# State-space stage: conditioning weights spread by 1 MB units over the rounds, x for the norms in 4 KB packets, a tile's outputs ahead of the next tile's lags

## Chip, cores and metric

One NeuronCore of a Trainium2 chip runs the kernel. The metric is device time in microseconds (us) of one execution, median of several runs. Engines: TensorE (PE), VectorE (DVE), ScalarE (ACT), GpSimd (POOL), and SyncE (SP), which only issues DMAs here.

## What is computed

Two transformer-like blocks over 256 tokens of width 2048, in f32. The change touches only the first mixer of the first block, a state-space layer, and the conditioning ahead of it:

```python
def adaln(cond, w, b):
    return jnp.split(jax.nn.silu(cond) @ w + b, 6, axis=-1)      # w_mod: 2048 x 12288
...
sh1, sc1, gt1, sh2, sc2, gt2 = adaln(c, w_mod[layer], b_mod[layer])
csh1, csc1, cgt1, csh2, csc2, cgt2 = adaln(c_ctx, w_mod[layer], b_mod[layer])
h_lat = modulate(rmsnorm(x_lat, norm_mix_pre[layer]), sh1[:, None], sc1[:, None])
h_ctx = modulate(rmsnorm(x_ctx, norm_mix_pre[layer]), csh1, csc1)
...
lam_bar, b_bar = s5_discretise(...)
st_ctx = s5_scan(uc_ctx, lam_bar, b_bar, s0, reverse)
st_lat = s5_scan(uc_lat, lam_bar, b_bar, s_ctx_final, reverse)
y_lat = y_lat + jnp.einsum('btgp,ghp->btgh', st_lat, c_mat).real   # both directions
```

`x_lat` (x) and `x_ctx` (ctx) have 256 rows each. The gelu of y_lat goes into the GLU matmul, and from there on the kernel is a sequence of large matmuls that the change leaves alone.

## The kernel before

**Tiles and rounds.** The 2048 channels are 16 tiles (KT) of 128. For each tile the recurrence is cut into chunks of L = 8 tokens: inside a chunk a Toeplitz matrix of lags (`tw`), between chunks a scan over states. Software pipeline, one tile per round: `for k in range(-1, KT)` on TensorE and ACT, `for k in range(KT)` on VectorE, `for n` on GpSimd and SP. Every engine's order is written out by hand, and semaphores tie them.

**One round on TensorE** (L1310 to L1340): `lag_blocks(k+1)` (L1247, needs GpSimd's `cpow` of tile k+1), `states(k+1)` (L1263), `outputs(k)` (L1277 with `tw`, L1280 with the states), two units of conditioning weights in `ada_rows` (L1188), `spread_modulation`, `select_c` (L1179), `transpose_x` (L1221), `output_transposes(k)` (L1290), two `transpose_e` (L1234) with two more units between them, and in rounds 0 to 3 four units more (`mod_rows`). `mod_columns` (L1199) turns a finished row of conditioning into columns.

**The others.** GpSimd: `powers_of_c(n)` (into `cpow`, two buffers; waits for `outputs(n-2)` through y_done) and `phases(n)` (into `pt`), all through the helper at L1841; before tile 2 it scales the remaining powers of lambda. VectorE: `rotate(k)` (phase rotation and scan, gives s_done), `copy_lags(k+1)` (L1717 to L1719, into `rw`), `finish`, in three rounds `modulation` (L1731 and neighbours), `powers_of_b(k+2)`; most through the helper at L1539. ACT: the gelu (L1454), PSUM copies, `modulate_u` (L1442), `normalise_x` (L1432), and it issues the weights of the rounds (L1078). SP: `toeplitz(n)` stores `rw` to DRAM (L1108), waits, and loads it back as `tw` by eight DMAs (L1113; `tw` has one buffer, so it also waits for `outputs(n-1)`), then loads C (L1099) and x (L1103) for tile n+3.

**Conditioning weights.** w_mod (2048 x 12288) comes as 24 blocks of 512 columns, each in 4 units of 1 MB ([128, 4, 512]), through the 4 slots of `raw`. Block 0 to 3 (16 units) are worked off ahead of the rounds, round -1 takes 4 units, rounds 0 to 3 take 8 each, rounds 4 to 14 take 4 each. A unit's load waits until the unit four earlier is used (ada_unit).

**Prologue.** `load_xs` brings x and ctx rows for the norms in two halves of four tokens, onto 64 partitions (32 for each of ctx and x, 8 KB runs); ACT squares them with accumulation (`square_x`, L1392, 8 instructions), VectorE and ACT make rstd_x from them. VectorE builds the lambda powers (lp_ready), `powers_of_b(0)`, the phase table ab[2,3], `modulation(0)`, a complex product (`cmul`), the table ab[0,1], and gives tables_ready (L1761), which GpSimd's `phases(0)` needs.

## Time and profile before

| | |
|---|---|
| median of 3 runs | 3557.34 us (3548.33 to 3568.26) |
| profiled execution: time, span | 3554.54 us, 3552.7 us |
| mean granted TensorE clock | 0.955 of 2.4 GHz |
| busy over the span | PE 3286.0 us (92%), DVE 2145.0 (60%), ACT 1380.7 (39%), POOL 480.5 (14%) |
| DMA | 643.22 MB, mean 181 GB/s |
| state-space stage | 0 to about 465 us |

The profile is one execution. The page gives totals over the whole span; the stage is some 13% of it, so its rows come from the trace, cut to stretches. L numbers are lines of the kernel before. In a row, "[3.73 <-PE acc L1247]" says that the engine sat idle for 3.73 us before it, and what ended that. A DMA's time to landing runs from its issue.

### The profile page before, as it was taken

To read this page: it belongs to the slowest core of one execution; us is meant where nothing else is said; L and a number is where in the kernel's file an instruction comes from. 1 tells how busy PE (TensorE), PEld (TensorE's weight loads), DVE (VectorE), ACT (ScalarE), POOL (GpSimd) and SP (SyncE) were. 2 spreads that over 40 slices of the span, in tenths; PEclk is the share of its full clock that TensorE was granted. 3 is DMA by queue.
4 is the path that set the end of the run, shared out by engine and by line. 5 is a ranking of instruction groups with operands and counts; after the bars stand their busy time and mean duration, and the time that the engine had idled before them with its cause. 6 is when DMAs were issued, how large, how long until landed. Compare 5 with 4: busy or idle time off the path is not lost.

```text
span 3552.7 us, 51801 instructions
## 1 busy us (share of the span) xinstructions
PE 3286.0 (92%) x21097; PEld 2763.3 (78%) x21097; DVE 2145.0 (60%) x1850; ACT 1380.7 (39%) x1385; POOL 480.5 (14%) x352
## 2 busy tenths in 40 slices
PE   5788899799999999886789999999999899999998
PEld 3445578688888888675678888888868788888887
DVE  7668755565555555699565555555644555555555
ACT  4446543433333333322234434433323344344332
POOL 2869900000000000096000000000000000000000
PEclk7888899899999999998799999999999999999999
DMA  9988875255555555344145555555524455555552
GB/s 299 305 282 257 260 243 175 91 184 189 185 189 182 190 186 189 107 142 148 36 154 178 186 190 182 186 189 189 177 92 142 142 186 184 187 187 189 189 183 89
DMA packets 351014, 643.22 MB, mean 181 GB/s; under 512 B 21599, under 2 KB 50359, under 8 KB 350519
## 3 DMA queue, kind: packets, MB, share of 16 engines
q1 hardware_dynamic: 309952, 561.68, 48.9%
q10 hardware_dynamic: 40951, 79.98, 6.6%
q8 instruction: 80, 1.31, 0.2%
q14 instruction: 31, 0.25, 0.0%
HBM read 637.54 MB, written 4.06 MB: 181 GB/s over the span
## 4 chain that ended last, share of the span: by engine, by line
PE 83%; DVE 6%; POOL 5%; issue 2%; DMA 2%; ACT 1%; SPq 1%; DVEq 1%; ACTq 0%; POOLq 0%
PE acc L439 49%; PE acc L440 25%; POOL cpow L1841 3%; DMA raw<-in_w_mod_dram 2%; POOL ptmp L1841 1%; PE acc L1263 1%; DVE z L943 1%; DVE w_lo L793 1%; PE acc L1280 1%; PE acc L521 1%; PE acc L533 1%; PE acc L464 1%; PE acc L1188 1%; PE acc L1247 1%; DVE hf L832 0%
## 5 line engine op out<-in xcount | busy, mean ns | idle before, releaser
L439 PE MATMUL acc<-xin,w_hi 128*128 128x512 f32 x5376 | 1915.2, 399 | 58.9 <-DVE xin L807 33.7
L793 DVE TENSOR_TENSOR w_lo<-raw,w_hi 128x2048 fp32r<-128x2048 f32 x484 | 1111.2, 2301 | 1079.0 <-ACT w_hi L640 1078.8
L440 PE MATMUL acc<-xin,w_lo 128*128 128x256 f32 x5376 | 1519.4, 283 | 0.0
L640 ACT ACTIVATE w_hi<-raw 128x2048 fp32r<-128x2048 f32 x484 | 926.8, 1917 | 1365.1 <-PE acc L440 1365.0
L439 PEld LDWEIGHTS acc<-xin,w_hi 128*128 128x128 f32 x5376 | 1017.2, 189 | 312.5 <-issue 35.6
L440 PEld LDWEIGHTS acc<-xin,w_lo 128*128 128x128 f32 x5376 | 1021.5, 190 | 0.0
L439 PE MATMUL acc<-hid,w_hi 128*128 128x512 f32 x2432 | 845.4, 392 | 0.0
L440 PE MATMUL acc<-hid,w_lo 128*128 128x256 f32 x2432 | 681.2, 280 | 0.0
L439 PEld LDWEIGHTS acc<-hid,w_hi 128*128 128x128 f32 x2432 | 455.1, 187 | 101.4
L440 PEld LDWEIGHTS acc<-hid,w_lo 128*128 128x128 f32 x2432 | 459.6, 189 | 0.0
L799 DVE TENSOR_REDUCE tmp<-acc 128x1024 f32<-128x2048 f32 x116 | 265.0, 2284 | 19.9 <-PE acc L440 19.9
L1188 PE MATMUL acc<-raw,cond 128*32 128x512 f32 x768 | 112.8, 700 | 45.5 <-DMA raw<-in_w_mod_dram 44.2
L674 ACT ACTIVATE hid<-tmp 128x1024 f32 x38 | 40.3, 1061 | 225.9 <-DVE tmp L863 131.1
L1064 POOL MEMSET y<- 128x4096 f32 x1 | 3.5, 3522 | 921.2 <-DVE xin L807 921.2
L1188 PEld LDWEIGHTS acc<-raw,cond 128*32 128x32 f32 x768 | 20.4, 119 | 106.0 <-DMA raw<-in_w_mod_dram 71.9
L1041 POOL MEMSET conv_in<- 128x120 f32 x1 | 0.2, 204 | 755.0 <-DVE xr L826 755.0
L943 DVE SCALAR_TENSOR_TENSOR z<-conv_in,par,z 128x256 f32<-128x256 f32 x180 | 101.1, 635 | 0.0
L1057 POOL TENSOR_SCALAR conv_tmp<-conv_in,par 128x256 f32<-128x256 f32 x60 | 88.5, 1475 | 0.0
L807 DVE TENSOR_TENSOR hid<-tmp,hid 128x1024 f32 x38 | 46.6, 1226 | 55.6 <-ACT hid L674 55.6
L1841 POOL TENSOR_TENSOR cpow<-cpow,ptmp 128x1024 f32<-128x1024 f32 x32 | 75.6, 2362 | 1.3
L1841 POOL TENSOR_TENSOR ptmp<-ct,lpc 128x1024 f32<-128x1024 f32 x32 | 62.0, 1936 | 70.6 <-PE acc L1280 47.1
L1442 ACT ACTIVATE u<-acc,modt 128x32 f32<-128x32 f32 x256 | 70.8, 417 | 0.7 <-PE acc L1221 0.2
(241 smaller groups left out, 2063.5 us busy)
## 6 DMA issues: line engine op xcount, KB each, us to landing
raw<-in_ffn_w_gate_dram SPq DMA_DIRECT2D x88, 1024.0 KB, 5.2
raw<-in_ffn_w_up_dram SPq DMA_DIRECT2D x88, 1024.0 KB, 5.1
raw<-in_ffn_w_down_dram SPq DMA_DIRECT2D x88, 1024.0 KB, 5.1
raw<-in_w_mod_dram ACTq DMA_DIRECT2D x76, 1024.0 KB, 9.7
raw<-in_w_mlp_in_dram SPq DMA_DIRECT2D x64, 1024.0 KB, 5.2
raw<-in_w_mlp_out_dram SPq DMA_DIRECT2D x64, 1024.0 KB, 5.1
raw<-in_s_w_glu_dram SPq DMA_DIRECT2D x32, 1024.0 KB, 5.3
raw<-in_ab_w_in_dram SPq DMA_DIRECT2D x32, 1024.0 KB, 5.3
```

The lines of the kernel that those rows point to most:

```text
L439: pe.matmul(bank, w_hi[:, slot, w], operand[:, kt, :], start=(kt == 0), stop=False)
L440: ins = pe.matmul(bank[:, 0:TOK], w_lo[:, slot, w], operand[:, kt, 0:TOK], start=False, stop=(kt == UK * units - 1))
L640: act.activation(w_hi[:, slot, :], raw[:, slot, :, :].rearrange("p k n -> p (k n)"), ACT.Copy).then_inc(hi_ready, 1)
L674: act.activation(hid[:, ds(CH * chunk, CH) if not isinstance(chunk, int) else slice(CH * chunk, CH * (chunk + 1)), 0:TOK], tmp[:, half], A ...
L793: dve.tensor_tensor(w_lo[:, slot, :], raw[:, slot, :, :].rearrange("p k n -> p (k n)"), w_hi[:, slot, :].bitcast(F32), SUB).then_inc(lo_re ...
L799: dve.tensor_reduce(dst, acc[:, 4 * half:4 * half + 4, :].rearrange("p a (t b) -> p a b t", t=2), AX.X, ADD).then_inc(folded, 1)
L807: return dve.tensor_tensor(dst[:, k, TOK:2 * TOK], src, dst[:, k, 0:TOK].bitcast(F32), SUB).then_inc(done, 1)
L943: dve.scalar_tensor_tensor(z[:, k, :], x, c, z[:, k, :], MUL, ADD).then_inc(conv_dve, 1)
L1057: pool.tensor_scalar(conv_tmp[:, step % 2, :], x, c, None, ALU.mult).then_inc(conv_mul, 1)
L1188: ins = pe.matmul(ps[0][32 * q:32 * q + 32, :], cond[:, kk * UK + q, window:window + 32], raw[:, kk, q, :], start=(m + kk == 0), stop=(kk ...
L1442: ins = act.activation(u[b][:, g, q * NCH:(q + 1) * NCH], ps[6][:, g * 64 + q * NCH:g * 64 + (q + 1) * NCH], ACT.Identity, bias=modt[:, 16 ...
L1841: return pool.tensor_tensor(o, x, y, op)
```

## The change

1. Blocks are numbered in one order (`ORDER`: eight for the modulation, then sixteen), and units are handed out one by one: 8 in the prologue, then 5 and 6 in turn in rounds -1 to 14 (`FIRST_UNIT`). In a round TensorE takes two units behind `states`, two between the two `transpose_e` and the rest behind the second. The loads are issued four units ahead. `mod_columns` of blocks 1 to 3 moves from rounds -1, 2, 4 to the head of rounds 1, 3, 5, and `modulation` to rounds 1, 3, 5.
2. x and ctx for the norms come in four DMAs of 1 MB onto 128 partitions, each partition one half-chunk of four tokens in runs of 4 KB, all ahead of the weights. ACT squares them in 4 instructions instead of 8, behind the copies of B. Two small matmuls bring the 128 sums to 64 partitions.
3. On TensorE `outputs(k)` stands ahead of `lag_blocks(k+1)` and `states(k+1)`.
4. Around it: C of tile 0 is loaded first and selected before the weights, `c_sel` waits ahead of `copy_modulation` go (the PSUM order is held by TensorE waiting for mod_raw), and VectorE builds the phase table ab[2,3] ahead of `powers_of_b(0)`.

The diff, cut to its core:

```diff
+        ss_x = whole("ss_x", [P, L // 2])
...
-        xs = Region(xin_at, xin_at + 32 * KB)("xs", [64, L // 2, D])
+        xs = Region(xin_at, xin_at + 32 * KB)("xs", [P, L // 2, D])
...
+        xwide = [v.rearrange("(c f j) d -> (c f) j d", f=2, j=L // 2) for v in (ctx2, x2)]
...
-        MOD = [(0, 1), (2, 3), (6, 8), (10, 12)]
-        ADA = [4, 5, 7, 9, 11] + list(range(13, 24))
-        BLOCK_COL = {MOD[b][v]: (1 - v) * D + b * UN for b in range(4) for v in range(2)}
-        BLOCK_COL.update({m: 2 * D + n * UN for n, m in enumerate(ADA)})
-
-        def ada_units(queue, m, units=range(UK)):
-            col = BLOCK_COL[m]
-            for k in units:
+        ORDER = [("mod", b, v) for b in range(4) for v in range(2)] + [("ada", n) for n in range(KT)]
+        BLOCK_COL = [2 * D + b[1] * UN if b[0] == "ada" else (1 - b[2]) * D + b[1] * UN for b in ORDER]
+        BLOCK_WINDOW = [15 - b[1] if b[0] == "ada" else 47 - (16 + 4 * b[1] + 2 * b[2]) for b in ORDER]
+        FIRST_UNIT = [8 + 11 * (r // 2) + 5 * (r % 2) for r in range(KT + 1)]
+        assert FIRST_UNIT[KT] == 4 * len(ORDER)
+
+        def ada_load(queue, first, last):
+            for i in range(first, min(last, 4 * len(ORDER))):
+                m, k = divmod(i, SLOTS)
                 if m:
-                    queue.wait_ge(ada_unit, 4 * m + (k - 3))
-                queue.dma_start(raw[:, k, :, :], w_mod[:, k * UK:(k + 1) * UK, col:col + UN]).then_inc(raw_ready[k], 16)
+                    queue.wait_ge(ada_unit, i - 3)
+                queue.dma_start(raw[:, k, :, :], w_mod[:, k * UK:(k + 1) * UK, BLOCK_COL[m]:BLOCK_COL[m] + UN]).then_inc(raw_ready[k], 16)
...
-            def load_xs(half):
-                for s in range(2):
-                    sp.dma_start(xs[s * NCH:(s + 1) * NCH, :, :], xch[s][:, 4 * half:4 * half + 4, :]).then_inc(xs_in, 16)
+            def load_xs():
+                for h in range(2):
+                    for s in range(2):
+                        sp.dma_start(xs[s * 64:(s + 1) * 64, :, h * (D // 2):(h + 1) * (D // 2)],
+                                     xwide[s][:, :, h * (D // 2):(h + 1) * (D // 2)]).then_inc(xs_in, 16)
...
-            load_xs(0)
-            ada_units(sp, 0)
             load_c(0)
+            load_xs()
+            ada_load(sp, 0, 4)
             load_x(0)
-            sp.wait_ge(xs_sq, 4)
-            load_xs(1)
-            ada_units(sp, 1)
-            ada_units(sp, 2)
+            ada_load(sp, 4, 8)
             sp.wait_ge(c_sel, 1)
             load_c(1)
-            ada_units(sp, 3)
             sp.wait_ge(xt_scaled, 1)
             load_x(1)
+            ada_load(sp, 8, 12)
             sp.wait_ge(c_sel, 2)
             load_c(2)
-            ada_units(sp, 4)
             sp.wait_ge(xt_scaled, 2)
             load_x(2)
...
-            def ada_rows(m, window, units=range(UK)):
-
-                for kk in units:
+            def ada_rows(first, last):
+
+                for i in range(first, last):
+                    m, kk = divmod(i, SLOTS)
                     pe.wait_ge(raw_ready[kk], 16 * (m + 1))
                     for q in range(UK):
-                        ins = pe.matmul(ps[0][32 * q:32 * q + 32, :], cond[:, kk * UK + q, window:window + 32], raw[:, kk, q, :],
-                                        start=(m + kk == 0), stop=(kk == UK - 1), skip_group_check=True)
+                        ins = pe.matmul(ps[0][32 * q:32 * q + 32, :], cond[:, kk * UK + q, BLOCK_WINDOW[m]:BLOCK_WINDOW[m] + 32],
+                                        raw[:, kk, q, :], start=(i == 0), stop=(kk == UK - 1), skip_group_check=True)
                     ins.then_inc(ada_unit, 1)
-
-            def mod_rows(b, v):
-                ada_rows(MOD[b][v], 47 - (16 + 4 * b + 2 * v))
...
-            mod_rows(0, 0)
-            mod_rows(0, 1)
+            pe.wait_ge(b_sb, 3)
+            select_c(0)
+            pe.wait_ge(xs_sq, 4)
+            pe.wait_ge(angle_ready, 1)
+            for f in range(2):
+                ins = pe.matmul(ps[2][0:64, 4 * f:4 * f + 4], sel_g[:, f * 64:(f + 1) * 64], ss_x[:, :], start=True, stop=True)
+            ins.then_inc(ss_tr, 1)
+            ada_rows(0, 8)
             pe.wait_ge(b_sb, 4)
+            pe.wait_ge(c_sb, 1)
             mod_columns(0)
-            select_c(0)
-            mod_rows(1, 0)
-            pe.wait_ge(c_sb, 1)
+            pe.wait_ge(mod_raw, 1)
+            select_c(1)
             spread_modulation(0)
-            select_c(1)
             transpose_x(0)
             transpose_e(0, 0)
             transpose_e(0, 1)
-            mod_rows(1, 1)
 
             for k in range(-1, KT):
-                if k + 1 < KT:
-                    lag_blocks(k + 1, (k + 1) % 2)
-                    states(k + 1, (k + 1) % 2)
+                if k in (1, 3, 5):
+                    mod_columns((k + 1) // 2)
                 if k >= 0:
                     outputs(k, k % 2)
+                    if k + 1 < KT:
+                        lag_blocks(k + 1, (k + 1) % 2)
                 if k + 1 < KT:
-                    if k in (-1, 2, 4):
-                        pe.wait_ge(ada_sb, {-1: 2, 2: 3, 4: 4}[k])
-                    ada_rows(ADA[k + 1], 15 - (k + 1), (0, 1))
-                if k in (-1, 2, 4):
-                    mod_columns({-1: 1, 2: 2, 4: 3}[k])
+                    states(k + 1, (k + 1) % 2)
+                    if k < 0:
+                        lag_blocks(0, 0)
+                    i0, i1 = FIRST_UNIT[k + 1], FIRST_UNIT[k + 2]
+                if k in (1, 3, 5):
+                    pe.wait_ge(mod_raw, (k + 3) // 2)
+                if k + 1 < KT:
+                    if k in (1, 3, 5):
+                        pe.wait_ge(ada_sb, (k + 3) // 2)
+                    ada_rows(i0, i0 + 2)
                 if k + 2 < KT:
                     spread_modulation(k + 2)
                 if k + 3 < KT:
@@ -1337,11 +1346,11 @@
                 if k + 2 < KT:
                     transpose_e(k + 2, 0)
                 if k + 1 < KT:
-                    ada_rows(ADA[k + 1], 15 - (k + 1), (2, 3))
+                    ada_rows(i0 + 2, i0 + 4)
                 if k + 2 < KT:
                     transpose_e(k + 2, 1)
-                if 0 <= k < 4:
-                    mod_rows(2 + k // 2, k % 2)
+                if k + 1 < KT:
+                    ada_rows(i0 + 4, i1)
                 if k == KT - 2:
...
+            def square_x():
+                act.wait_ge(xs_in, 64)
+                for j in range(L // 2):
+                    act.activation(xs[:, j, :], xs[:, j, :], ACT.Square, accum_out=ss_x[:, j:j + 1]).then_inc(xs_sq, 1)
...
-            square_x(0)
             copy_b(2)
             copy_b(3)
+            square_x()
...
             copy_lam_powers(0)
-            square_x(1)
-            copy_adarow(0, MOD[0][1])
-            copy_modulation(0)
             copy_c(0, 0)
             act.wait_ge(ss_ready, 1)
             act.activation(rstd_x[:, :], rstd_x[:, :], ACT.Sqrt).then_inc(rstd_root, 1)
+            copy_adarow(0, 8)
+            copy_modulation(0)
             act.wait_ge(rstd_ready, 1)
             normalise_x(0)
...
-            copy_adarow(1, MOD[1][1])
 
             for k in range(-1, KT):
                 if k >= 0:
                     if k + 1 < KT:
                         act.wait_ge(s_done, k + 1)
                         copy_r8(k + 1)
+                    if k in (1, 3, 5):
+                        copy_modulation((k + 1) // 2)
                     if k == KT - 1:
                         act.wait_ge(bd_sb, KT)
                         act.wait_ge(bpow_done, KT)
@@ -1505,29 +1513,30 @@
                 if k + 2 < KT:
                     act.wait_ge(k_done, k + 2)
                     block_diagonal_b(k + 2)
-                if k in (-1, 2, 4):
-                    copy_modulation({-1: 1, 2: 2, 4: 3}[k])
                 if k + 2 < KT:
                     copy_spread(k + 2)
                 if k + 3 < KT:
                     copy_c(k + 3, (k + 3) % 2)
                 if k + 2 < KT:
                     modulate_u(k + 2, k % 2)
-                    ada_units(act, ADA[k + 1] + 1, (0, 1))
+                    i = FIRST_UNIT[k + 1]
+                    ada_load(act, i + 4, i + 6)
                 if k >= 0:
                     copy_output(k)
                 if k + 2 < KT:
                     copy_e(k + 2)
-                    ada_units(act, ADA[k + 1] + 1, (2, 3))
+                    ada_load(act, i + 6, i + 8)
                 if k + 3 < KT:
                     copy_lam_powers(k + 3)
                     normalise_x(k + 3)
-                if 0 <= k < 4:
-                    ada_units(act, ADA[k + 1] + 2)
-                if k in (1, 3):
-                    copy_adarow(2 + k // 2, MOD[2 + k // 2][1])
+                if k + 2 < KT:
+                    ada_load(act, i + 8, FIRST_UNIT[k + 2] + 4)
                 if k == KT - 2:
-                    copy_adarow(4, ADA[KT - 1])
+                    ada_load(act, FIRST_UNIT[k + 1] + 4, FIRST_UNIT[k + 2])
+                if k in (0, 2, 4):
+                    copy_adarow(1 + k // 2, FIRST_UNIT[k + 2])
+                if k == KT - 2:
+                    copy_adarow(4, FIRST_UNIT[KT])
...
+            powers([ab[:, 2], ab[:, 3]], uu, L)
+            dve.wait_ge(ss_tr, 1)
+            dve.tensor_scalar(rstd_x[:, :], ps[2][0:64, 0:L], 1.0 / D, EPS, MUL, ADD).then_inc(ss_ready, 1)
             powers_of_b(c0, 0)
-            dve.wait_ge(xs_sq, 8)
-            dve.tensor_scalar(rstd_x[:, :], rstd_x[:, :], 1.0 / D, EPS, MUL, ADD).then_inc(ss_ready, 1)
-            powers([ab[:, 2], ab[:, 3]], uu, L)
...
-                if k in (0, 3, 5):
-                    modulation(cm, {0: 1, 3: 2, 5: 3}[k])
+                if k in (1, 3, 5):
+                    modulation(cm, (k + 1) // 2)
```

## Rows read from the trace of the kernel before

**Rows 1.** Chain that ended last, one late round: start us, us, what.

```profile
403.26 1.93 POOL ptmp L1841
...
415.78 1.08 PE acc L1247 x32
...
424.22 1.93 POOL ptmp L1841
```

**Rows 2.** Stretches between lag blocks; columns as in the first line.

```profile
core 0: us, PE busy (x) PEld busy (x) DVE busy (x) ACT busy (x) POOL busy (x), PEclk, DMA share, GB/s
107.80:139.56 31.76, 23.40 (x298) 13.28 (x299) 19.00 (x35) 13.10 (x40) 30.97 (x24) 0.77 0.93 291
139.56:167.93 28.37, 22.14 (x305) 13.25 (x309) 16.61 (x32) 12.47 (x39) 25.53 (x18) 0.86 0.87 296
167.93:200.79 32.86, 25.03 (x312) 13.67 (x308) 16.60 (x32) 13.66 (x42) 18.90 (x12) 0.76 0.97 319
200.79:230.51 29.72, 23.32 (x305) 12.72 (x301) 17.17 (x36) 13.10 (x40) 18.91 (x12) 0.79 0.91 293
230.51:250.42 19.91, 18.34 (x274) 13.06 (x267) 16.61 (x32) 11.56 (x36) 12.70 (x7) 0.86 0.90 297
250.42:436.73 186.31, 151.65 (x2378) 107.63 (x2378) 152.32 (x292) 116.68 (x358) 170.07 (x108) 0.89 0.85 256
```

**Rows 3.** Waits, 139.56 to 230.51 us: us in total, times, longest us.

```profile
PE acc L1188 <- DMA raw<-in_w_mod_dram: 18.5, 10, 3.1
```

**Rows 4.** Timeline, TensorE: start us, us, instruction; outputs(1) and the units behind it.

```profile
144.59 0.42 PE L1277 MATMUL acc<-tw,u 128*32 128x128 f32 x8
...
147.32 1.92 PE L1188 MATMUL acc<-raw,cond 128*32 128x512 f32 x16
```

**Rows 5.** Timeline, VectorE: the lag copies of two rounds.

```profile
396.45 0.27 DVE L1717 COPY rw<-acc 128x112 f32<-128x112 f32 x1 [3.33 <-PE acc L1247]
...
416.93 0.28 DVE L1717 COPY rw<-acc 128x112 f32<-128x112 f32 x1 [3.73 <-PE acc L1247]
```

**Rows 6.** Timeline, SP queue: issue of one tile's eight loads of tw.

```profile
406.84 4.21 SPq L1113 DMA_DIRECT2D tw<-r_scratch  x8
```

**Rows 7.** DMA issues, single rounds: KB each, median us to landing; a slow and a quick one.

```profile
r_scratch<-rw SPq DMA_DIRECT2D x1, 120.0 KB, 9.2
r_scratch<-rw SPq DMA_DIRECT2D x1, 120.0 KB, 5.7
tw<-r_scratch SPq DMA_DIRECT2D x8, 64.0 KB, 6.7
tw<-r_scratch SPq DMA_DIRECT2D x8, 64.0 KB, 2.5
```

**Rows 8.** Timeline, VectorE: first and last instruction of one modulation.

```profile
252.61 0.56 DVE L1539 TENSOR_TENSOR msum<-mraw,par 128x8 f32<-128x8 f32 x1
...
254.24 1.32 DVE L1539 TENSOR_TENSOR mrhs<-mcol,s5c 128x128 f32<-128x128 f32 x1
```

**Rows 9.** Timeline, VectorE in the prologue.

```profile
22.29 0.69 DVE L1539 TENSOR_TENSOR tv<-tv 128x128 f32<-128x128 f32 x3
...
56.20 0.16 DVE L1753 TENSOR_SCALAR rstd_x<-rstd_x 64x8 f32<-64x8 f32 x1 [8.56 <-ACT xs L1392]
...
66.96 0.20 DVE L1756 RECIPROCAL rstd_x<-rstd_x 64x8 f32<-64x8 f32 x1 [2.06 <-ACT rstd_x L1481]
...
71.26 4.93 DVE L1539 TENSOR_TENSOR tv<-ab,tv 128x128 f32<-128x128 f32 x4
76.11 2.58 DVE L1539 TENSOR_TENSOR tv<-tv,tv 128x128 f32<-128x128 f32 x2
...
87.54 0.23 DVE L1761 COPY tv<-tv 128x128 f32<-128x128 f32 x1
```

**Rows 10.** DMA issues: the load issued at 5.5 us.

```profile
xs<-in_x_dram SPq DMA_DIRECT2D x1, 1024.0 KB, 18.5
```

**Rows 11.** Timeline, TensorE: first matmul of the GLU.

```profile
465.07 0.77 PE L439 MATMUL acc<-xin,w_hi 128*128 128x512 f32 x1
```

11 lines of the change are left out of this document (3 added, 8 removed).

## The prediction, made before the change was run

> **What bounds the kernel now.** The change touches only the state-space stage, which ends at 465 us of 3552.7, so I read that stage alone. First the chain of waits: in the late rounds it repeats one loop [rows 1]. GpSimd builds the powers of C (403.26 to 415.78, 12.5 us), then TensorE runs `lag_blocks`, `states` and `outputs`, and only `outputs` frees the buffer for GpSimd's next powers (424.22). Second the table of stretches, cut where each tile's `lag_blocks` starts [rows 2]. The first full round (31.76 us) has GpSimd busy for 30.97: it also scales the remaining powers. The next three rounds carry 8 units of conditioning weights each and last 28.37, 32.86 and 29.72 us, together 90.95, at 293 to 319 GB/s. The ten behind them carry 4 units each: 19.91, then nine in 186.31 us (20.7 each) at 256 GB/s, with GpSimd 18.9 us busy per round. Third the waits of the three heavy rounds: TensorE waits for weights, ten times [rows 3]. So before: heavy rounds wait for loads, light ones for GpSimd's loop.
>
> **Units spread.** Eight of sixteen units leave the prologue, and 16 rounds take 5 and 6 in turn, 5.5 on average. Nothing is added or dropped in all. The three heavy rounds should fall to even ones; the price is that ten light rounds grow by 1.5 units. A unit is 8 matmuls, 0.96 us [rows 4], so 1.4 us of TensorE in each, which costs nothing where it stands in TensorE's idle time ahead of the next rotation's end, and 1.4 where that is gone.
>
> **Outputs ahead of the next lags.** GpSimd's loop loses its TensorE part (8.4 us from 415.78 to 424.22), since the buffer is now freed before `lag_blocks`. GpSimd alone would allow its busy 18.9 us a round. But what is late next? VectorE works in order: rotate, `copy_lags`, finish, powers of B, next rotate. `copy_lags` needs `lag_blocks`, and that now stands behind `outputs`, which needs the end of the rotation. Before, VectorE sat idle for 3.73 us of its 20.48 at this place [rows 5], for GpSimd, and worked 16.75. Now it sits idle for `outputs` (144.59 to 147.32, 2.75 us [rows 4]), `lag_blocks` (1.08, row 415.78) and two hand-overs of 0.1: 4.0 us. Its loop is then 16.75 + 4.0 = **20.8 us**, no shorter than the light rounds of before. This is the floor of a round, whatever GpSimd could do.
>
> **The lag matrix's way through DRAM.** `copy_lags` starts `toeplitz` on SP's queue: store, wait, eight loads into `tw`, and `outputs` of the same tile waits for them. Before, it had a round plus the time of `lag_blocks` and `states`. Now it has to close inside one round: `outputs` and lags 3.9, copy 0.8, store 5.7 to 9.2, issue of eight loads 4.2, landing 2.5 to 6.7 [rows 6, 7], the higher figures where weights are in flight. That is 17.1 us with idle DMA engines and 24.8 with busy ones. In a round of 5.5 units the engines are idle for a part only, about from 8 to 12 us behind the start of `outputs`, so I take 21 to 22. SP's other issues (C, x) stand between the `tw` loads and the next store as before; what they wait for (selection of C, scaling of x) ends inside the round, so they hold back no store.
>
> **Bytes of a round.** A light round moves 256 GB/s x 20.7 us = 5.3 MB, of which 4.2 are its 4 units; the other 1.1 MB stay. With 5.5 units it is 6.9 MB. The three heavy rounds reached 296, 319 and 293 GB/s [rows 2] with the same four slots; 6.9 MB at 319 is 21.6 us, at 303 (their mean) 22.8. I take **T = 21.8 us**, between the floor of 20.8 and 22.8 and nearest to the best heavy round, since even rounds leave fewer gaps.
>
> **Conditioning columns.** Three rounds (k = 1, 3, 5) now have VectorE's `modulation` (252.61 to 255.56, 3.0 us [rows 8]) on the loop that sets the round, and `mod_columns` ahead of `outputs` on TensorE, behind an ACT copy that waits for the last unit of the round before; whatever is queued on TensorE, `outputs` first, waits with it. Before, two of the three stood under the idle VectorE of a heavy round. I take 3.7 us for each; the bounds are 1.5 and 6. From the lags of tile 2 to those of tile 15: 10 x 21.8 + 3 x 25.5 = 294.5, against 90.95 + 19.91 + 186.31 = 297.2 before: **-2.7 us**. With T = 20.8 it is 281.5 (-15.7); with T = 24.2 it is 325.1 (+27.9).
>
> **Prologue.** What sets its end is VectorE's chain to the two phase tables (ready at 87.5 [rows 9]), then GpSimd without a pause: phases, powers of C, scaling, powers of C, lags of tile 2. On VectorE's chain the change removes the wait for the squares, 8.6 us (56.20), and that for the root, 2.1 (66.96). `modulation` and the product behind it no longer run beside GpSimd's powers of C: six multiplications of [128,128] took 7.4 us there (71.26 to 78.7), 0.23 each alone (22.29), so with their gaps -5.5, and -1.3 for `modulation`. Against it: C is selected early now, so GpSimd's 12.5 us fall onto the first phase table, 18 multiplications with both operands in SBUF, 8.8 us alone (78.7 to 87.5, the second table, is the same work). At the pace of row 71.26, 1.2 us for one, some 11 pass in GpSimd's 12.5 us where 25 would have: +9. And ACT squares all of x ahead of the parameter copy for which VectorE waits: +2. Sum -10.7 - 5.5 - 1.3 + 9 + 2 = **-6.5 us**; bounds -13 (half the collision) and +1 (the whole table waits GpSimd out). The first eight units set nothing: the last four are issued from about 42 us, and 4.2 MB at 300 GB/s are in by 56, ahead of the chain's need for them at 66. The x loads bring 4.2 MB ahead of all weights. An old one of 1 MB onto 32 partitions, at 5.5 us in the queue, landed 18.5 us later, at 24.0 [rows 10]; with B's 2.1 MB and its twin ahead of it, 4.3 MB came in the 20 us from 4 us on, 215 GB/s. At that rate the new 4.2 MB land at 34 us, at the heavy rounds' 300 GB/s at 25 to 28; the squares, four instead of eight, are done at 42 or 36, and both are inside the +2 and its bounds.
>
> Here the Trainium skill speaks against the new shape (SBUF — State Buffer, Door 1: The DMA port swizzle): partitions 0 to 63 reach no more ports than 0 to 31, so a [64, N] load is as slow as a [32, N] one. By that rule the squares are done at 42 and the sum of the prologue is about -4.5; by the heavy rounds' rate it is -8.
>
> **Tail.** From the lags of tile 15 to the first matmul of the GLU were 28.3 us (436.73 to 465.07 [rows 11]). `tw` of the last tile no longer waits for `outputs` of the one before (-4 us), but the last round has 6 units, whose last two are issued late and hold back `ada_columns`, the last `outputs` behind it and two slots of the GLU, and ACT still converts two GLU slots ahead of the last gelu. I take **-1**, bounds -4 and +4.
>
> **Sum.** -6.5 - 2.7 - 1 = -10.2 against the profiled execution's own 3554.5 us (span 3552.7), that is 3544.3. The median of the runs shown is 2.8 us above it; some of that is chance, so I say **3545**. Nothing behind the stage is touched.
>
> **Rivals.**
> (a) The loads hide and VectorE's loop of 20.8 us is all: -6.5 - 15.7 - 1 = -23, 3532. For it: the light rounds move only 256 GB/s, so there is room. Against: rounds at 293 to 319 GB/s all waited for weights.
> (b) Slower: the lag matrix's way through DRAM becomes the loop. Place: the wait for `tw` ahead of `outputs`. Price: T = 24.2, with store and landing near 9 and 6, gives +27.9 - 6.5 - 1 = +20, 3575. It makes the kernel slower from T = 22.6 on. For it: in late light rounds the store took 9.2 and the landing 6.7 already with 4 units. Against: a round's first weights are issued only 12 us behind `outputs`, when the store is mostly done.
> (c) The prologue gives nothing since the phase table waits for GpSimd, and T is 22 (297.1 for the 13 rounds): 0, 3555. For it: row 71.26. Against: GpSimd has only six instructions there. The Trainium skill (SBUF — State Buffer, Who interferes with whom) calls the port that both share an exclusive lock, held for a whole instruction; by that rule row 71.26 is the pace for any such pair, and the trace agrees.
> (d) The change doesn't free GpSimd, since the next powers still wait for something that `outputs` stood behind: then T stays near 20.7 to 21, which is case (a) in time.
>
> **How the numbers follow.** Forecast (T from 21.2 to 22.6, -20 to +3 us): 0.45. (a) with (d): 0.30. (b): 0.13. (c): 0.12. Half a per cent (17.8 us) is about what a measurement of this kernel can tell from no change. Faster by more: most of (a), 0.25, and the low end of the forecast, 0.09: 0.34. Slower by more: most of (b), 0.12. Same: 0.54. The range takes in (a) with the prologue at its best (-33, 3522) and (b): 3522 to 3576.
>
> **What the profile would show.** Right: rounds of 21 to 23 us with no steps of 30 among them, GpSimd no longer waiting for `outputs`, VectorE's wait for `lag_blocks` near 4 us a round, DMA near 310 GB/s from 130 us on, tables ready near 81 us and the lags of tile 2 near 133. Rounds of 24 us with `outputs` waiting for `tw` would mean (b); of 20.8, (a). Wrong in kind: a first phase table of 8.8 us beside GpSimd's powers, or TensorE at its lower clock through `outputs`, which would add up to 2.8 us to every round.

## The result and the profile after

The changed kernel takes **3597.3 us** (median; 3595.4 to 3600.5) against 3555.7 for the kernel before: ratio 1.0114, 95% interval 1.0089 to 1.0138. It is slower by 41.6 us, where 3545 was forecast, and the time lies above the range. The profiled executions have spans of 3593.8 and 3552.7 us. Their 41.1 us lie here (starts of `lag_blocks` and of the first GLU matmul in both traces; sums rounded):

```
                                   before    after    forecast   came out
to the lags of tile 2              139.56   135.18       -6.5       -4.4
lags of tile 2 to lags of tile 15  297.17   321.88       -2.7      +24.7
lags of tile 15 to the GLU          28.34    30.68       -1         +2.3
GLU to the end                    3087.63  3106.06        0        +18.4
```

So two terms failed: the rounds, and one that the forecast did not have at all. First the rounds. The table of stretches of the changed kernel, cut at the lags of each tile, with the same columns as [rows 2]; the last row is all 13 rounds:

```profile
266.09:290.48 24.39, 20.13 (x287) 12.54 (x283) 16.61 (x32) 13.13 (x40) 18.90 (x12) 0.86 0.97 288
290.48:314.54 24.06, 19.08 (x278) 12.30 (x274) 16.61 (x32) 13.09 (x40) 18.90 (x12) 0.86 1.02 304
314.54:338.50 23.96, 19.97 (x286) 12.67 (x283) 16.61 (x32) 13.17 (x40) 18.93 (x12) 0.86 0.92 275
135.18:457.06 321.88, 255.60 (x3614) 160.99 (x3610) 228.56 (x428) 169.32 (x513) 251.29 (x161) 0.84 0.91 273
```

From tile 7 on the rounds are even (22.8 to 24.5 us), as meant, but at 24 us: three above the light rounds of before. Ahead of that they take 23.9 to 27 us, and one takes 30.0. VectorE (16.6) and GpSimd (18.9) work no more per round than before; both wait. For what, the chain of waits says (start, us, what); this is the round from 290.55:

```profile
289.13 1.42 PE acc L1279 x32
290.55 1.05 PE acc L1246 x32
...
292.24 6.09 DMA r_scratch<-rw
...
298.35 0.33 SPq L1118
...
301.95 8.23 DMA tw<-r_scratch
...
310.32 0.60 PE acc L1276 x8
310.92 1.86 PE acc L1279 x32
312.79 0.58 PE acc L1276 x8
313.37 1.25 PE acc L1279 x32
314.61 1.01 PE acc L1246 x32
```

Lags (L1246) 1.05, copies 0.64, store 6.09, issue of the eight loads 3.6 (298.35 to 301.95), landing 8.23, `outputs` (L1276, L1279) 4.3, and lags again: 24.06 us with the short gaps, and every step of it is the lag matrix's way through DRAM or stands directly behind it. This is rival (b) of the prediction, even in its figure of 24.2. In the next round the chain runs over weights instead (`322.91 10.46 DMA raw<-in_w_mod_dram`).

### The profile page after: what moved, and what is told of

Read it like the earlier page. It is cut to its first block, busy times and chain, and to the rows that moved or that the text cites. A ratio compares the mean times of both kernels' runs of the same rounds, so it can differ in the third digit from the quotient of the medians.

```text
span 3593.8 us, 51799 instructions
## 1 busy us (share of the span) xinstructions
PE 3317.9 (92%) x21101; PEld 2772.3 (77%) x21101; DVE 2152.7 (60%) x1850; ACT 1375.9 (38%) x1377; POOL 480.4 (13%) x352
## 4 chain that ended last, share of the span: by engine, by line
PE 82%; DVE 7%; DMA 5%; issue 3%; ACT 2%; SPq 1%; DVEq 1%; ACTq 0%
PE acc L441 49%; PE acc L442 25%; DMA raw<-in_w_mod_dram 2%; PE acc L1279 1%; DVE z L945 1%; DMA tw<-r_scratch 1%; DVE w_lo L795 1%; PE acc L466 1%; DMA r_scratch<-rw 1%; PE acc L523 1%; PE acc L535 1%; PE acc L1190 1%; DMA xs<-in_x_dram 1%; DVE bpow L1548 1%; DVE acc L1548 1%
## 5 line engine op out<-in xcount | busy, mean ns | idle before, releaser
L441 PE MATMUL acc<-hid,w_hi 128*128 128x512 f32 x2432 | 859.7, 399 | 0.0
L801 DVE TENSOR_REDUCE tmp<-acc 128x1024 f32<-128x2048 f32 x116 | 265.0, 2284 | 20.9 <-PE acc L442 20.9
L1233 PE MATMUL acc<-consts,bpow 128*128 128x128 f32 x256 | 48.3, 350 | 38.3 <-DVE bpow L1548 34.3
L1233 PEld LDWEIGHTS acc<-consts,bpow 128*128 128x128 f32 x256 | 38.5, 181 | 56.0 <-DVE bpow L1548 35.7
```

The source lines that it names most:

```text
L441: pe.matmul(bank, w_hi[:, slot, w], operand[:, kt, :], start=(kt == 0), stop=False)
L801: dve.tensor_reduce(dst, acc[:, 4 * half:4 * half + 4, :].rearrange("p a (t b) -> p a b t", t=2), AX.X, ADD).then_inc(folded, 1)
L1233: ins = pe.transpose(ps[3 + 2 * (q % 2)][:, r * P:(r + 1) * P], bpow[:, ri, cb, :], ident)
```

## Experiments

The stretches of all kernels, read like those above (late rounds: mean of the seven from tile 8 to tile 15):

```
                 13 rounds  late   tail   GLU to end
before             297.2    20.6   28.3   3087.6
changed            321.9    23.8   30.7   3106.1
after_layout       325.3    23.8   30.8   3090.9
order_old          292.5    22.1   34.7   3088.6
outputs_first      330.1    22.3   23.7   3088.0
light_new          291.5    20.7   24.2   3088.1
light_old          259.2    19.4   25.7   3088.1
no_way             295.7    20.9   31.5   3090.6
prologue16         277.0    20.9   28.2   3094.6
best2              277.6    21.0   27.9   3056.3
```

### Where the GEMMs lost 18 us: moved arrays

No instruction of the GEMMs changed. The new `ss_x` takes 32 bytes per partition ahead of `work_at`, so `w_hi`, `w_lo` and `hid`, the arrays of the GEMMs, all moved by 32 bytes.

**after_layout**:

```diff
-        ss_x = whole("ss_x", [P, L // 2])
...
         mrhs = s5("mrhs", [P, KT, 32])
+        ss_x = s5("ss_x", [P, L // 2])
```

> The changed kernel with one difference: the new array ss_x (16 bytes per partition, taken as 32) is placed inside the stage's own region, so that everything behind work_at, hid among it, lies where it lay before the change. Theory (address): the 18.4 us that the GEMMs lost come from hid having moved by 32 bytes; then the matmuls on hid take 391 ns again instead of 395 to 403, the part from the first GLU matmul to the end is 3088 us as before instead of 3106, and the time is about 3578 (3597 less 18 or 19), 22 above before. Rival (program layout, or the clock): the matmuls on hid stay near 399 ns and the time at 3597. The stage itself, 487.7 us to the first GLU matmul, is the same under both.

Measured: 3584.8 us, 12.5 below the changed kernel; GLU to end 3090.9, 15 less, and the median of the matmuls on hid is 391 ns again. The stage, expected to stay the same, was 5 us longer in this trace (rounds 325.3 for 321.9), so differences of 3 or 4 us over the 13 rounds are not read below.

**before_pad32** (the reverse):

```diff
+        whole("pad32", [P, 8])
         work_at = whole.at
```

> The kernel before with an unused 32 bytes per partition ahead of work_at, no instruction changed. Theory (address): the stage keeps its 465 us, the matmuls on hid go from 391 to about 399 ns, and the time rises by 18 us, to 3574. Rival (program layout or clock): nothing changes, 3556.

Measured: 3572.2 us, ratio 1.0040 (1.0025 to 1.0054), GLU to end 3106.9. An unused array of 32 bytes reproduces most of the loss: 19 us of the traces from the GLU to the end, 15 of the medians. Groups of TensorE (busy us, mean ns; idle; groups overlap, so their times do not add up to a stretch): first the kernel before with the pad, then with w_hi alone moved, which is told below. The kernel before has 1915.2, 1519.4, 845.4 and 681.2 us in these four groups.

```profile
L440 PE MATMUL acc<-xin,w_hi 128*128 128x512 f32 x5376 | 1920.1, 401 | 57.6 <-DVE xin L808 33.8 <-DVE w_lo L794 23.9
L441 PE MATMUL acc<-xin,w_lo 128*128 128x256 f32 x5376 | 1521.6, 283 | 0.0
L440 PE MATMUL acc<-hid,w_hi 128*128 128x512 f32 x2432 | 859.7, 399 | 0.0
L441 PE MATMUL acc<-hid,w_lo 128*128 128x256 f32 x2432 | 684.0, 281 | 0.0
```

```profile
L440 PE MATMUL acc<-xin,w_hi 128*128 128x512 f32 x5376 | 1887.0, 397 | 56.2 <-DVE xin L808 33.7 <-DVE w_lo L794 22.5
L441 PE MATMUL acc<-xin,w_lo 128*128 128x256 f32 x5376 | 1502.8, 280 | 0.0
L440 PE MATMUL acc<-hid,w_hi 128*128 128x512 f32 x2432 | 843.6, 391 | 0.0
L441 PE MATMUL acc<-hid,w_lo 128*128 128x256 f32 x2432 | 681.0, 280 | 0.0
```

Which array? **before_xin32** puts a pad of 32 bytes ahead of xin and another ahead of `work_at`; **xin_last** places xin last:

```diff
-        xin_at = whole.at
-        xin = whole("xin", [P, KT, 2 * TOK], F32R)
...
         rstd_x = whole("rstd_x", [64, L])
+        xin_at = whole.at
+        xin = whole("xin", [P, KT, 2 * TOK], F32R)
         work_at = whole.at
```

> The kernel before with xin 32 bytes further on and hid 32 bytes past a multiple of 64 as it was, no instruction changed. Theory (address, 32 past a multiple of 64 is the faster place of a moving operand for whatever array): the 4800 matmuls on xin go from 399 to 391 ns, and the time falls by about 38 us, to 3518. Rival (it is something about hid alone, or not the address): no change, 3556.

Measured: 3573.1 us, GLU to end 3104.5: slower, not faster. The theory that "32 past a multiple of 64" is the good place fell; here w_hi, w_lo and hid had moved by 64 bytes.

> The kernel before with xin placed behind consts, par, ada and rstd_x instead of ahead of them; nothing behind it moves, and no instruction changes. hid, whose matmuls took 391 ns, begins 3488 bytes into a stretch of 4096; xin now begins there too, and with 32 bytes moved either way both had taken 399. Theory (the place of the moving operand within a few hundred or thousand bytes sets its pace, whatever array it is): the 5376 matmuls xin,w_hi go from 399 to 391 ns, hid stays at 391, and the time falls by about 38 us, to 3518. Rival (something that only the products of hid have, their place against w_hi and w_lo or the work beside them): xin stays at 399 ns and the time at 3556.

Measured: 3542.4 us, ratio 0.9976 (0.9955 to 0.9998), GLU to end 3072.8, 15 below before. The gain is there, though less than half of what was expected: hid rose from 392 ns in the mean to 394, xin fell only from 399.5 to 397.6, 17 us of busy time. The gain is not steady: eight of the ten executions took 3540 to 3552 us, two 3568. The four small arrays that stood behind xin moved too.

**hid32**, **w_lo32**, **w_hi32**: the kernel before with one array moved (in w_lo32 hid moves with w_lo).

```diff
+        gm("pad32", [P, 8])
         hid_at = gm.at
```

> The kernel before with 32 unused bytes between w_lo and hid: hid and all behind it move, w_hi, w_lo, xin and the whole stage stay. Theory H (it is the place of hid): its matmuls go from a median of 391 ns to 398, xin stays at 392. Theory W (it is the place of the weights w_hi and w_lo, for in every kernel in which they moved the matmuls on xin rose too, from a median of 392 to 397, though xin lay still): both stay at 391 and 392.

Measured: 3552.5 us, GLU to end 3092.2; hid at a median of 390 ns, xin at 395. Hid's own place is not it.

```diff
+        gm("pad32", [P, 8])
         w_lo = gm("w_lo", [P, SLOTS, UK * UN], F32R)
```

> The kernel before with 32 unused bytes between w_hi and w_lo: w_lo, hid and all behind them move, w_hi, xin and the stage stay. hid's own place is already known to make no difference. Theory A (the place of w_lo sets the pace): the matmuls of hid on w_hi go from a median of 391 ns to 398, and the part from the first GLU matmul to the end from 3088 us to 3105. Theory B (the place of w_hi): they stay at 391 ns and 3088 us.

Measured: 3531.6 us, GLU to end 3064.7: 23 us less than before, which neither theory had.

```diff
-        gm = Region(work_at, whole.end)
+        gm = Region(work_at - 32, whole.end)
         w_hi = gm("w_hi", [P, SLOTS, UK * UN], F32R)
+        gm("pad32", [P, 8])
         w_lo = gm("w_lo", [P, SLOTS, UK * UN], F32R)
```

> The kernel before with w_hi alone 32 bytes nearer to the start (over rstd_x, which is dead by then), w_lo, hid, xin and the stage where they were. Theory (the place of w_hi carries the 18 us): the matmuls of hid on w_hi go from a median of 391 ns to 398 and the part from the first GLU matmul to the end from 3088 us to about 3105. Rival (it is the places of w_hi and w_lo taken together, and what counts is that they differ or are both moved): 391 ns and 3088 us or less, perhaps the 3065 of w_lo32.

Measured: 3528.8 us, GLU to end 3060.2. The rival holds: moving either array alone by 32 bytes *gains* 23 to 27 us, moving both together, by 32 or by 64, loses 17 to 19. It is their places taken together that count. Both gains come from the same distance: w_lo32 moves w_lo up, w_hi32 moves w_hi down, and both make 32800 bytes out of the 32768 from the start of w_hi to that of w_lo. Other distances were not run. Distance alone does not decide either, since with 32768 bytes the times are 3088 in one place and 3105 in two others. The groups above show where the time sits: some 28 us less busy time in the xin, w_hi group than before, and 17 in xin, w_lo. Ten kernels with xin, w_hi and w_lo placed as before had 3087.6 to 3094.6 us from the GLU to the end, so seven microseconds are scatter and these differences are not. Why the pair matters is not settled. hid32, w_lo32 and w_hi32 are single executions; best2, below, repeats the gain of w_lo32 in four executions.

### Why the rounds take 24 us

**order_old** undoes one part in after_layout, the order on TensorE:

```diff
+                if k + 1 < KT:
+                    lag_blocks(k + 1, (k + 1) % 2)
+                    states(k + 1, (k + 1) % 2)
                 if k >= 0:
                     outputs(k, k % 2)
-                    if k + 1 < KT:
-                        lag_blocks(k + 1, (k + 1) % 2)
-                if k + 1 < KT:
-                    states(k + 1, (k + 1) % 2)
-                    if k < 0:
-                        lag_blocks(0, 0)
```

> The changed kernel with ss_x placed as in after_layout and with TensorE's order of before in the rounds: lags of the next tile and its states first, then the outputs. The new spread of the units, the new prologue and the place of the modulation stay. Theory (the way of the lag matrix through DRAM is closed into a loop by outputs standing ahead of the lags): the 13 rounds from tile 2 to tile 15 take about 297 us as before instead of 322, and the time is 25 us below after_layout. Rival (bytes: 71.5 units instead of 64 lie in those 13 rounds, and the weights bound them): the rounds stay at 24 us, 322 in all, and the time is that of after_layout within 5 us.

Measured: 3555.7 us, ratio to before 0.9996 (0.9986 to 1.0005); 29 below after_layout. The 13 rounds take 292.5 us. Its stretches, rounds of 5 and 6 units in turn:

```profile
271.54:291.88 20.34, 17.84 (x279) 12.10 (x271) 16.60 (x32) 12.08 (x37) 14.56 (x8) 0.90 0.98 305
291.88:316.69 24.81, 18.16 (x282) 11.13 (x286) 16.60 (x32) 13.96 (x44) 23.43 (x17) 0.93 1.02 305
316.69:336.67 19.98, 17.49 (x278) 11.74 (x270) 16.61 (x32) 12.06 (x37) 14.41 (x8) 0.92 1.00 312
```

Against the changed kernel, the seven rounds of five units fall from 171.4 us to 144.3, the six of six units only from 150.4 to 148.2: the order costs where weights do not bind. And the way is as slow here as there: from tile 8 on, the medians of store and landing were 5.2 and 6.9 us in the changed kernel, and here they are

```profile
raw<-in_w_mod_dram ACTq DMA_DIRECT2D x39, 1024.0 KB, 10.4
tw<-r_scratch SPq DMA_DIRECT2D x56, 64.0 KB, 6.0
r_scratch<-rw SPq DMA_DIRECT2D x7, 120.0 KB, 7.8
```

(issues, KB each, us to landing). They cost nothing, and TensorE waits for `tw` not once in these 13 rounds, because the lags of a tile start ahead of `outputs` of the tile before, and the matrix has a whole round to come back.

**outputs_first** is that part alone, in the kernel before:

```diff
-                if k + 1 < KT:
-                    lag_blocks(k + 1, (k + 1) % 2)
-                    states(k + 1, (k + 1) % 2)
                 if k >= 0:
                     outputs(k, k % 2)
+                if k + 1 < KT:
+                    lag_blocks(k + 1, (k + 1) % 2)
+                    states(k + 1, (k + 1) % 2)
```

> The kernel before with one part of the change alone: in every round TensorE works the outputs of tile k ahead of the lags and states of tile k+1. Spread of the units, prologue and modulation stay as before. Theory (the order closes store, landing, outputs and lags into one loop): the light rounds, 20.5 us before, become 22.5 to 24, those from tile 6 to tile 15 cost 20 to 35 us in all, and the time is 3580 to 3590. Rival (the order costs only when five or six units a round slow the store and the landing): the light rounds stay within 1 us of 20.5 and the time within 8 us of 3556.

Measured: 3591.6 us, ratio 1.0101 (1.0084 to 1.0117); the 13 rounds 330.1 us against 297.2. Even with four units only three of the seven late rounds take 20.7 us, the others 22.3 to 25.3. The order alone costs 35 us, 33 of them in the rounds; the even spread does not rescue it.

**light_new, light_old** take the traffic away, **no_way** the lag matrix's way (in the last, DVE's, TensorE's and SP's waits for the later trips are cut to the first as well):

```diff
-                queue.dma_start(raw[:, k, :, :], ... BLOCK_COL[m]:BLOCK_COL[m] + UN])
+                n = UN if i < 8 else UN // 8
+                queue.dma_start(raw[:, k, :, 0:n], ... BLOCK_COL[m]:BLOCK_COL[m] + n])
```

```diff
                 sp.wait_ge(r_sb, n + 1)
+                if n:
+                    sp.wait_ge(y_done, n)
+                    return
```

> after_layout with an eighth of the bytes of each weight unit from the ninth on (64 of 512 columns are loaded; most of the conditioning is computed from old data, so that part of the computation is left out; the instructions are the same in number and size). Theory (the loop's length is the traffic's doing: store and landing of the lag matrix take 6 to 8 us each beside loads of 1 MB): both fall to 3 us or so, and the rounds to about 20 us, set by VectorE or GpSimd. Rival (the loop is long by itself, waits and issues): the rounds stay above 22 us without the traffic.

> order_old with the same eighth of the bytes (most of the conditioning is left out). Theory: in that order weights bound only the rounds of six units (23.9 us) and GpSimd those of five (20.3), so every round comes to 20.3 or a little less, and the 13 rounds to about 262 us instead of 292. Rival (the long rounds wait for something other than weights): 24 and 20 go on alternating.

> after_layout with all weights, but the lag matrix is stored and loaded for tile 0 alone; the later outputs take tile 0's (that part of the computation is left out, the matmuls are the same). Theory: in the changed kernel the rounds of five units (24.5 us in the mean) wait for store and landing, those of six (25.1) for weights; without the way through DRAM the first fall to about 20.7, the pace that the same order had without traffic, and the second to 23 or 24, so the 13 rounds come to 285 to 295 us instead of 325. Rival (it is the traffic of the weights or the lower clock behind TensorE's waits that hold both): they stay above 310.

Measured, 13 rounds: light_new 291.5 us, light_old 259.2, no_way 295.7, with all three theories (no_way 0.7 above its range). Each is a single execution. One late round of light_new (store 2.1 us, landing 2.6), light_old and no_way:

```profile
281.15:301.82 20.67, 18.68 (x278) 11.57 (x274) 16.61 (x32) 13.03 (x40) 18.93 (x12) 0.83 0.37 84
```

```profile
276.50:295.81 19.31, 16.85 (x282) 10.85 (x282) 16.61 (x32) 13.01 (x42) 18.94 (x12) 1.00 0.38 91
```

```profile
283.26:303.94 20.68, 17.66 (x279) 11.49 (x275) 16.61 (x32) 13.12 (x40) 18.91 (x12) 0.92 0.96 328
```

Three readings. With the outputs first, 20.67 us is the floor of a round, and the forecast's 20.8 was right: from one `lag_blocks` to the next the chain of waits of this round of light_new is VectorE's work, then `outputs`. With the lags first it is 19.31, GpSimd working without a pause (18.94): the reordering *raised* the floor it was meant to lower. And no_way holds 20.68 us in this round at 328 GB/s, and 20.9 in the mean of the late rounds at 296 GB/s, with all the weights: with the outputs first, neither the traffic nor the way through DRAM costs more than 0.3 us of a late round by itself, only the way while traffic slows it. The rounds of six units fell as well (I had expected 23 to 24), so their wait for weights in the changed kernel was a consequence too; the units landed in 7.5 us in the median there instead of 10.4.

The four kernels together say more. The order costs 32 us of the 13 rounds with little traffic too (291.5 against 259.2), as much as with all of it (325.3 against 292.5), and traffic costs some 33 in either order: with the outputs first by the lag matrix's way, with the lags first by TensorE's waits for weights (33.8 us in order_old). So the round trip is where the forecast went wrong, but without it the reordering would still have been a loss.

The early rounds of light_new are longer, which traffic cannot explain: 24.0, 25.8, 24.6, 26.4, 24.6 and 21.2 us, then 20.7. Its timeline at the one that ends at 235.36:

```profile
225.97 0.87 DVE L1549 TENSOR_TENSOR st<-turned,acc 128x128 f32<-128x128 f32 x4
...
229.47 0.57 ACT L1397 ACTIVATE adarow<-acc 128x512 f32<-128x512 f32 x1
...
230.10 1.05 PE L1199 MATMUL acc<-s5c,adarow 128*128 128x4 f32 x8 [2.56 <-ACT adarow L1397]
...
231.08 0.43 PE L1277 MATMUL acc<-tw,u 128*32 128x128 f32 x8
231.44 1.81 PE L1280 MATMUL acc<-cpow,st 64*32 64x128 f32 x32
233.18 0.65 PE L1277 MATMUL acc<-tw,u 128*32 128x128 f32 x8
233.76 1.67 PE L1280 MATMUL acc<-cpow,st 64*32 64x128 f32 x32
235.36 0.86 PE L1247 MATMUL acc<-cpow,bd 128*32 128x128 f32 x24
```

The rotation is done at 226.84, but `mod_columns` (L1199) stands ahead of `outputs` and waits for ACT's copy (L1397); the outputs begin 4.2 us late, and take 4.3 us instead of 2.75: behind the 2.56 us in which TensorE stood still, the granted clock is 0.65 of 2.4 GHz from 231 to 233 and 0.58 from 233 to 235.4, that is at the 1.2 GHz level for most of the outputs. In the round behind it VectorE has 20.48 us of work instead of 16.61, for `modulation`.

### The prologue

**c_late** is order_old with C of tile 0 selected late, as before:

```diff
             pe.wait_ge(b_sb, 3)
-            select_c(0)
             pe.wait_ge(xs_sq, 4)
...
-            pe.wait_ge(c_sb, 1)
             mod_columns(0)
+            pe.wait_ge(mod_raw, 1)
+            select_c(0)
+            pe.wait_ge(c_sb, 1)
```

(ACT's `copy_c(0, 0)` moves behind `copy_modulation(0)` with it.)

> order_old with C of tile 0 selected after the columns of the first modulation, as in the kernel before, so that GpSimd's powers of C no longer fall onto VectorE's first phase table. Theory (the collision costs 10.9 us there, 19.7 instead of 8.8, and the powers of C would fall onto bpow and modulation, which read PSUM or are short, for less): the first table takes 9 to 10 us, the tables are ready at 73 to 76 us instead of 82, the lags of tile 2 come 4 to 8 us earlier than order_old's 133.9, and the time is 3550. Rival (another wait takes its place: the squares or the root, the columns of the modulation, whose units are in by 56 us): the tables are ready at 80 or later, and lags of tile 2 and time stay within 2 us of order_old's (133.9 and 3556).

Measured: 3559.2 us, ratio to before 1.0006 (0.9996 to 1.0016). The rival's outcome, and only in part by its mechanism: the first table did take 7.8 us (44.4 to 52.2) instead of 19, but then VectorE waited 3.95 us (until 64.06) for the columns of the modulation, as the rival said, and GpSimd's powers fell onto the product and the second table, whose first three multiplications took 2.1 to 2.6 us each instead of 0.4. The tables were ready at 85.9 instead of 82, the lags of tile 2 at 137.5 instead of 133.9. In both places tried, the twelve microseconds of GpSimd beside a table have a price.

### Versions that keep what is good

**prologue16** is order_old with 16 units in the prologue and fewer at the end; **best1** adds xin_last, **best2** w_lo32 as well:

```diff
+        FIRST_UNIT = running sums of [16, 6, 7] + [5] * 11 + [4] * 3
...
-            ada_load(sp, 4, 8)
+            ada_load(sp, 4, 12)
             sp.wait_ge(c_sel, 1)
             load_c(1)
+            ada_load(sp, 12, 16)
             sp.wait_ge(xt_scaled, 1)
             load_x(1)
-            ada_load(sp, 8, 12)
             sp.wait_ge(c_sel, 2)
             load_c(2)
+            ada_load(sp, 16, 20)
...
             mod_columns(0)
+            ada_rows(8, 12)
...
             transpose_e(0, 1)
+            ada_rows(12, 16)
```

> order_old with 16 of the 96 weight units in the prologue instead of 8, while the queues are idle there (2 GB/s from 60 to 70 us, 145 from 70 to 80), and 6, 7, eleven times 5 and three times 4 in the rounds. Theory (in order_old weights bound the rounds of six units alone, and GpSimd the rest): every round comes to 19.5 to 20.5 us, the 13 rounds to 262 to 268 instead of 292.5; the tail falls from 34.7 to about 28; the time is 3525. Rival (early units hold up C and x of the first tiles, or weights bound the rounds of five units too): the prologue grows by 5 or more, the rounds stay at 22, and the time is not under 3545.

Measured: 3543.4 us, ratio 0.9961 (0.9944 to 0.9977), between theory and rival. The rounds fell by 15.5 us, not by 27, and the tail by 6.5, but the prologue grew by 8.4 (lags of tile 2 at 142.3): the early units do hold it up.

> prologue16 with xin behind consts, par, ada and rstd_x, as in xin_last. Theory: both gains add up, for they lie in different parts of the kernel: 14 us below prologue16, 3511. Rival (xin_last's 14 us, with an interval of 1 to 16, were mostly scatter): the same time as prologue16 within 4 us.

> best1 with w_lo 32 bytes further on. Theory (the places of w_lo and of xin act each by itself): the part from the first GLU matmul to the end falls from 3075 us to about 3055, and the time to 3506. Rival (both moves give the same gain once): 3065 to 3075, and the time is that of best1, 3520 to 3526.

Measured: best1 3526.1 us, ratio 0.9928 (0.9901 to 0.9955); best2 3506.7 us, ratio **0.9857** (0.9834 to 0.9879). The gains add up, GLU to end 3075.2 and 3056.3 (best1's theory named 3511 only because it counted on 3525 for prologue16). best2 beats the kernel before by 1.4%, 51 us; 37 of them (prologue16 to best2) are placement.

## Why the prediction was wrong, step by step

**Way of the lag matrix: the step that failed.** "In a round of 5.5 units the engines are idle for a part only, about from 8 to 12 us behind the start of `outputs`, so I take 21 to 22." Of its two sums the busy one, 24.8, was right. The idle one, 17.1, took 5.7 for a store that was itself read beside weights: in light_new the way takes 10.0 us from the start of the lags (281.22) to the last landing (291.26), 12.8 with `outputs`. What failed is how much of the way lies in the idle part: it was taken as part, and was next to none. `outputs` begins at 286.26 here. Two-microsecond stretches of the changed kernel from there on:

```profile
286.00:288.00 2.00, 2.00 (x43) 1.46 (x40) 0.00 (x0) 0.62 (x1) 0.00 (x0) 0.63 1.05 384
288.00:290.00 2.00, 2.00 (x40) 1.16 (x36) 0.00 (x0) 0.00 (x0) 0.00 (x0) 0.51 1.06 382
290.00:292.00 2.00, 2.00 (x68) 1.60 (x62) 0.38 (x3) 1.34 (x4) 1.24 (x1) 1.00 1.09 322
292.00:294.00 2.00, 2.00 (x62) 1.63 (x62) 2.00 (x6) 0.99 (x3) 2.00 (x2) 1.00 1.09 321
294.00:296.00 2.00, 2.00 (x28) 0.82 (x22) 1.97 (x4) 0.00 (x0) 2.00 (x2) 1.00 1.05 385
296.00:298.00 2.00, 2.00 (x32) 1.86 (x27) 1.97 (x4) 1.48 (x7) 2.00 (x2) 1.00 0.95 352
298.00:300.00 2.00, 0.92 (x9) 0.81 (x8) 1.93 (x4) 2.00 (x9) 1.92 (x2) 1.00 0.39 73
300.00:302.00 2.00, 1.51 (x7) 1.51 (x8) 2.00 (x4) 2.00 (x8) 1.92 (x2) 0.55 0.98 322
```

The last units of the round before keep the DMA engines full (last two columns: share and GB/s) until 298, 12 us behind the start of `outputs`. The store of 292.2 lies wholly in that. They are mostly idle from 298 to 300 alone (0.39), and by then the next two units have been issued, at 298.3 and 298.7, beside the first `tw` load at 298.35. So both transfers meet traffic: 6.1 and 8.2 us. Rival (b) was given 0.13 because "a round's first weights are issued only 12 us behind `outputs`, when the store is mostly done". The 12 us are exact (286.26 to 298.26) and the store was done (298.33), but the units of the round before were forgotten for the store, and the landing was forgotten for the next ones. With traffic the 13 rounds cost 30.4 us more than light_new's; 13 had been taken (21.8 - 20.8 a round). That is 17.4 of the 27.4 us by which the rounds missed the forecast; the columns, below, are 11.7, the floor -1.7.

**Bytes of a round: right, and not the limit.** 273 GB/s over 321.88 us are 6.8 MB a round, for 6.9 forecast. But the 21.6 to 22.8 us that the text gave them, and from which T = 21.8 came, was not what bound: no_way moves the same units in 20.9 us in the mean of the late rounds.

**Floor of 20.8 us: right** (20.67). But the text said that the floor was "no shorter than the light rounds of before" and did not draw the conclusion that the reordering had then nothing to give. The reason is in the same sentence: VectorE waits for `outputs` ahead of `lag_blocks`. By light_old the old order has 19.31.

**Freed GpSimd (a, d):** GpSimd still waits for `outputs` in the changed kernel, 62.8 us in 11 waits over the 13 rounds. The forecast's sign, GpSimd no longer waiting for `outputs`, did not come. It was no longer what set the round, so that cost nothing.

**Columns: right in place, half in size.** Taken at 3 x 3.7 = 11.1 us, bounds 1.5 and 6 each; so it lies above its bounds. Without traffic the 13 rounds exceed 13 x 20.67 by 22.8 us: VectorE's `modulation` came out at the size taken, 3.9 in each of two clean rounds (184.35 and 235.36 of light_new), but `mod_columns` ahead of `outputs` added 5.2 and 5.8 in the rounds ahead of these, lower clock included. The text had both mechanisms and one price for the two.

**Outputs at the lower clock: partly.** Named as wrong in kind with up to 2.8 us a round. In the chain above they take 4.3 us where [rows 4] had 2.75, 1.5 more. It is a follower of the wait: where TensorE need not wait (light_old, granted clock 1.00 in the round shown) it is absent. But it is no small part. Of the 13 `outputs` between the lags of tile 2 and those of tile 15, nine took 4.1 to 4.6 us in the changed kernel, 13.4 us more in all than at 2.8: four directly behind a wait for `tw` of 2.6 to 3.9 us, three behind one for weights of 2.2 to 2.7, two behind `mod_columns`. In light_new only the last two did, 3.0 us more. So some 10 of the 30.4 us by which traffic lengthened the rounds are TensorE at the 1.2 GHz level behind the wait for `tw` or weights, a term that T = 21.8 had at nothing.

**Prologue: right in sum, with errors that cancel.** The lags of tile 2 came 4.4 us earlier, for 6.5 forecast, inside -13 to +1; the tables were ready at 82.0 for 81. The waits for squares and root went, -10.7 as forecast; the product gave -5.8 for -5.5, `modulation` -3.6 for -1.3. Against it the chain started 3.5 us later (43.37 for 39.87) behind ACT's squares, where +2 was taken, and the collision cost 10.9. Behind the tables 1.3 us were lost again: `mod_columns` and `outputs` now stand ahead of the lags of tile 2 (135.2, where order_old has 133.9). The x loads and the phase table:

```profile
33.98 1.91 ACT L1401 ACTIVATE xs<-xs 128x2048 f32<-128x2048 f32 x1 [5.33 <-DMA xs<-in_x_dram]
...
44.11 2.00 DVE L1548 TENSOR_TENSOR ab<-ab 128x128 f32<-128x128 f32 x1
46.03 2.14 DVE L1548 TENSOR_TENSOR lpt<-ab 128x128 f32<-128x128 f32 x1
```

They landed at 34.0 us, which is the 215 GB/s of the old load of half as many partitions, not the 300 of the heavy rounds: 218 GB/s from 14 to 24 us and 219 from 24 to 34, with the DMA engines full (1.03), and 387 from 34 to 42, when the weights on 128 partitions follow. The squares were done at 41.7. The Trainium skill (SBUF — State Buffer, Door 1: The DMA port swizzle) had said that 64 partitions load no faster than 32, and the trace agrees. The lower two rows are the phase table beside GpSimd's powers (43.94 to 56.94): it took 19.7 us (43.4 to 63.1) for the 8.8 that it takes alone, +10.9 where +9 was taken, at 2.0 to 2.5 us for one multiplication, so that six were done in GpSimd's time and not 11. The +9 was lucky: 11 multiplications in 12.5 us and the other seven at 0.49 make 16 us, which is +7. The exclusive port of the Trainium skill (SBUF — State Buffer, Who interferes with whom) fits this; the price per multiplication is above the 1.2 us of the row that I went by.

**Tail: wrong sign, inside its bounds.** 30.7 us for 27.3. The last round's six units are the cause, as its text feared: the last one lands at 474.8, `ada_columns` follows at 477.5 and `outputs` at 479.3. The -4 for the order was right: outputs_first, with four units, has 23.7 where before has 28.3. The six units cost 7 more (30.7), where 3 had been taken. With the lags first it is 28.2 with four units (prologue16) and 34.7 with six (order_old).

**GEMMs: no term at all.** "Nothing behind the stage is touched" was true of instructions and false of addresses. after_layout shows the edit without it: 3584.8 us, above the range too, and slower than before by 0.7% (0.5 to 0.9).

**Rival (b): the right mechanism, at 0.13.** Its price has a slip: 13 rounds of 24.2 and three times 3.7 are 325.7 us, not 325.1. By the text's own terms T = 21.2 and 22.6 give -18 and 0, not -20 and +3. Neither changes the outcome.

## What to carry to other kernels

When an instruction is moved ahead of another, follow everything that its delay starts, through every queue, and ask whether the way now closes inside one round: here a wait that had a whole round to spare became the round, and the pause that it put ahead of the outputs also lowered TensorE's clock in them. A transfer's time on such a way has to be read beside the traffic that the changed kernel will have at that moment, issue by issue, not averaged over a round. And a change that allocates a few bytes moves every array behind it: compare the busy time of untouched matmuls, or pad the layout, before a difference of half a per cent is given to the edit.

## What the runs showed of the hardware

- The pace of long series of f32r matmuls depends on where the two weight arrays lie: from the GLU to the end 3060 and 3065 us with one of them moved by 32 bytes away from the other, 3088 to 3095 as before, 3106 and 3107 with both moved by 32, 3105 with both moved by 64. Moving xin by 3360 bytes gave 3073, and with w_lo moved too 3056. The runs give no rule for it.
- Medians from tile 8 to tile 15: a store of 120 KB took 2.1 us in light_new and 2.7 in light_old, beside loads of 128 KB, and 5.2 (changed kernel) to 7.8 (order_old) beside loads of 1 MB; a load of 64 KB, one of eight, 2.6 and 2.5, and 6.9 to 6.0.
- `outputs` took 2.8 us at a granted clock of 1.00 (light_old) and 4.1 to 4.6 behind TensorE's waits of the changed kernel (0.63 and 0.51 in the two stretches from 286 to 290).
